# Gathering the first expert block's rows inside the routing block, and reordering the first pieces of the expert stage

## What is computed

```python
logits = h @ router_w + router_b
top_logit, top_e = lax.top_k(logits, 4)
top_w = softmax(top_logit)
# rows are sorted by expert and cut into blocks of 128 (each of one expert)
xb = h[buf_tok].reshape(n_blocks, 128, 1024)
def expert_block(xe, e):
    gate = minimum(xe @ w_gate[e] + b_gate[e], 7)
    up = clip(xe @ w_up[e] + b_up[e], -7, 7)
    act = (up + 1) * (gate * sigmoid(1.702 * gate))
    return act @ w_down[e] + b_down[e]
y = yb[dest] * sorted_w            # and summed back by token
x = x + g_m * moe(h)
```

## Time and profile before

| | |
|---|---|
| median of three runs | 2950.21 us |
| the profiled execution | 2950.6 us, its span 2948.8 us |
| TensorE busy | 2872.8 us (97% of the span) |
| VectorE busy | 2019.7 us (68%) |
| ScalarE busy | 1600.1 us (54%) |
| GpSimd busy | 551.3 us (19%) |
| expert stage | from 1680 us to the end |
| rate of the DMA engines in the expert stage | 381 to 388 GB/s in nearly every fortieth of the span |

### The profile page before, as it was taken

One profiled execution on the slowest core, in us unless ns is written; L12 is line 12 of the kernel. 1 busy time (PEld: TensorE's weight loads), 2 busy tenths in 40 slices (PEclk: granted clock), 3 DMA queues, 4 the chain that ended last, 5 costly groups with the idle time before them and its releaser, 6 DMA issues. The chain is left out here.

```text
span 2948.8 us, 41411 instructions
## 1 busy us (share of the span) xinstructions
PE 2872.8 (97%) x14988; PEld 2295.8 (78%) x14988; DVE 2019.7 (68%) x2273; ACT 1600.1 (54%) x1749; POOL 551.3 (19%) x479
## 2 busy tenths in 40 slices
PE   8999999998999999999999899999999999999999
PEld 4688888764788888876777688888888888888887
DVE  8642224587622236836753699999999999999998
ACT  5342323345522224434532577777777777777775
POOL 1012100113112100003100122322222222222331
PEclk9999999998999999999999999999999999999999
DMA  8422222220032232110022699999999999999995
GB/s 351 168 83 110 100 90 82 90 80 38 30 128 86 100 114 93 58 72 1 1 86 86 220 415 383 382 386 386 387 386 386 386 386 386 381 385 383 381 382 221
DMA packets 88924, 638.88 MB, mean 217 GB/s; under 512 B 10448, under 2 KB 11664, under 8 KB 26096
## 3 DMA queue, kind: packets, MB, share of 16 engines
q1 hardware_dynamic: 78592, 599.97, 51.9%
q0 software_dynamic: 9936, 36.75, 4.6%
q10 hardware_dynamic: 288, 0.65, 0.1%
HBM read 611.28 MB, written 26.05 MB: 216 GB/s over the span
## 5 line engine op out<-in xcount | busy, mean ns | idle before, releaser
L3208 DVE TENSOR_TENSOR arena_rounded<-arena,arena_rounded 128x2048 fp32r<-128x2048 f32 x420 | 951.1, 2286 | 90.6 <-ACT arena_rounded L3204 89.1
L3204 ACT ACTIVATE arena_rounded<-arena 128x2048 fp32r<-128x2048 f32 x420 | 801.3, 1918 | 209.4 <-PE banks L265 133.9
L263 PE MATMUL banks<-arena_rounded,operand_rounded 128*128 128x512 f32 (+1 forms) x2064 | 817.6, 396 | 4.2 <-DVE small_rounded L3500 2.2
L264 PE MATMUL banks<-arena_rounded,operand_rounded 128*128 128x512 f32 (+1 forms) x2064 | 801.6, 388 | 0.0
L265 PE MATMUL banks<-arena_rounded,operand_rounded 128*128 128x512 f32 (+1 forms) x1504 | 583.1, 388 | 0.0
L263 PEld LDWEIGHTS banks<-arena_rounded,operand_rounded 128*128 128x128 f32 x2064 | 387.8, 188 | 85.8 <-issue 4.7
L264 PEld LDWEIGHTS banks<-arena_rounded,operand_rounded 128*128 128x128 f32 x2064 | 388.1, 188 | 76.6 <-issue 1.0
L265 PEld LDWEIGHTS banks<-arena_rounded,operand_rounded 128*128 128x128 f32 x1504 | 282.4, 188 | 58.8
L263 PE MATMUL banks<-operand_rounded,arena_rounded 128*128 128x512 f32 (+2 forms) x712 | 268.0, 376 | 5.3 <-PE banks L265 5.2
L264 PE MATMUL banks<-arena_rounded,arena_rounded 128*128 128x512 f32 (+1 forms) x688 | 266.1, 387 | 0.0
L265 PE MATMUL banks<-operand_rounded,arena_rounded 128*128 128x512 f32 (+2 forms) x712 | 264.4, 371 | 0.0
(11 more groups left out here) (519 smaller groups left out, 3866.9 us busy)
## 6 DMA issues: line engine op xcount, KB each, us to landing
arena<-in_gate SPq DMA_DIRECT2D x140, 1024.0 KB, 7.5
arena<-in_up SPq DMA_DIRECT2D x140, 1024.0 KB, 7.7
arena<-in_down SPq DMA_DIRECT2D x140, 1024.0 KB, 6.1
arena<-in_dense SPq DMA_DIRECT2D x62, 2048.0 KB, 7.6
arena<-in_dense SPq DMA_DIRECT2D x6, 1024.0 KB, 5.1
small<-in_rows SPq DMA_DIRECT2D x7, 512.0 KB, 7.6
resid<-in_x SPq DMA_DIRECT2D x4, 512.0 KB, 8.2
expert_sums<-operand SPq DMA_DIRECT2D x4, 512.0 KB, 3.7
```

What stands on the lines that cost most here:

```text
L263: nc.tensor.matmul(out, left[0], right[0], start=start, stop=False)
L264: nc.tensor.matmul(out, left[0], right[1], start=False, stop=False)
L3204: nc.scalar.activation(high[q % NHI], raw[:, q, :], ACT.Copy).then_inc(high_ready, 1)
L3208: nc.vector.tensor_tensor(low[q], raw[:, q, :], high[q % NHI].bitcast(F32), ALU.subtract).then_inc(low_ready, 1)
```

## The change

- The semaphore of the first gather is made in the layout (`rows_in`), and `gather_rows` becomes a function of the module that takes the column as an argument.
- In `route`, VectorE writes `token` first and signals it with `numbered`; `filler` and `home` follow. GpSimd, at the end of its routing stream, waits for this and for the stores of the rows (`rows_out`), and gathers with `token`'s first column. In the expert stage it no longer loads `column`, copies `token_col` or gathers.
- ScalarE in the expert stage: `take_high` of piece 0, the four copies, both halves of `x_high`, then `take_high` of piece 1, then the one-element sigmoid with its table load, then piece 2.
- VectorE in the expert stage: `take_low` of piece 0 stands between the second and the third copy of bias sums.
- Two of the routing's semaphores become one (`weight`); counts on `staged` fall by one. TensorE's and SyncE's streams are unchanged but for the semaphore's name.

```diff
@@ route, vector
         dve.wait_ge(entered, ST)
         value = k.psum[:, 0, 0:P]
+        V.tensor_scalar(e["token"], value, float(S), float(S - 1), ALU.add, ALU.min).then_inc(numbered, 1)
         then(V.tensor_scalar(filler, value, 0.0, k.cst("pad"), ALU.is_equal, ALU.mult))
         V.scalar_tensor_tensor(out=e["home"], in0=value, scalar=float(S), in1=filler, op0=ALU.add, op1=ALU.add)
-        V.tensor_scalar(e["token"], value, float(S), float(S - 1), ALU.add, ALU.min)
@@ route, gpsimd
             i.then_inc(halved, 1)
+        pool.wait_ge(numbered, 2)
+        pool.wait_ge(rows_out, 16 * (ST + 1))
+        gather_rows(e, pool, e["token"][:, 0:1])
@@ experts, gpsimd
             last = last_block(pool)
-            column = pool.value_load(plan[0:1, NP:NP + 1], min_val=0, max_val=P - 1)
-            nc.gpsimd.tensor_copy(e["token_col"][:, 0:1], e["token"][:, bass.ds(column, 1)]).then_inc(staged, 1)
             nc.gpsimd.tensor_copy(e["choice"], k.cst("pick")[:, 0:1].broadcast_to([P, CAP])).then_inc(chosen, 1)
-            pool.wait_ge(staged, 1)
-            gather_rows(pool)
             pool.wait_ge(sums_out, 16 * ST)
@@ experts, scalar
-            nc.scalar.activation(table, table, ACT.Sigmoid).then_inc(y_ready, 1)
-            for q in range(2):
-                take_high(act, 0, q)
+            take_high(act, 0, 0)
             for t in range(ST):
                 act.wait_ge(biased, 2 * t + 1)
                 nc.scalar.activation(half(first_rows[t], 0), k.psum[:, first_bank(0, t), :], ACT.Copy).then_inc(biases_act, 1)
@@
             nc.scalar.activation(half(e["x_high"], 1), half(x_banks, 1), ACT.Copy).then_inc(x_high_ready, 1)
+            take_high(act, 0, 1)
+            nc.scalar.activation(table, table, ACT.Sigmoid).then_inc(y_ready, 1)
             for q in range(2, AHEAD):
                 take_high(act, 0, q)
@@ experts, vector
-            take_low(dve, 0, 0)
             for t in range(ST):
+                if t == ST // 2:
+                    take_low(dve, 0, 0)
                 dve.wait_ge(biased, 2 * t + 2)
                 V.tensor_copy(half(first_rows[t], 1), k.psum[:, first_bank(1, t), :]).then_inc(biases_dve, 1)
```

More of the change, by code:

```diff
@@ L2661, in expert_layout @@
     e["bias_in"] = k.nc.alloc_semaphore(name="expert_biases_in")
+    e["rows_in"] = k.nc.alloc_semaphore(name="expert_rows_in")
     e["in"] = [k.nc.alloc_semaphore(name=f"expert_weights_in_{n}") for n in range(PIECES)]
@@ L2670, in load_expert_piece, with gather_rows @@
     sp.dma_start(e["raw"][:, q, :], src[expert, half, part]).then_inc(e["in"][q], 16)
+def gather_rows(e, pool, column):
+    pool.indirect_dma_start(e["x_rows"], None, e["tokens_dram"],
+                            bass.IndirectOffsetOnAxis(ap=column, axis=0)).then_inc(e["rows_in"], 16)
 def route(k, e, fed):
@@ L2714, in route @@
     tokens = lambda t: slice(t * P, (t + 1) * P)
-    names = ("parts", "taken", "logits", "chain", "exp", "empty", "member", "ranked", "marked", "entered", "more", "more_turned",
+    names = ("parts", "taken", "logits", "chain", "weight", "empty", "member", "ranked", "marked", "entered", "more", "more_turned",
              "spread", "spread_turned", "spread_high", "rows_out", "turned_back", "copied",
-             "numbered", "halved", "weighed", "shared", "apart", "slotted", "bias_up", "bias_zero", "bias_high", "bias_low", "bias_out")
-    (parts_s, taken, logits_s, chain, exped, empty, member_s, ranked, marked, entered, more_s, more_turned,
+             "numbered", "halved", "shared", "apart", "slotted", "bias_up", "bias_zero", "bias_high", "bias_low", "bias_out")
+    (parts_s, taken, logits_s, chain, weight_s, empty, member_s, ranked, marked, entered, more_s, more_turned,
      spread_s, spread_turned, spread_high, rows_out, turned_back, copied,
-     numbered, halved, weighed, shared, apart_s, slotted, bias_up, bias_zero, bias_high, bias_low, bias_out) = (k.sem(f"route_{n}") for n in names)
+     numbered, halved, shared, apart_s, slotted, bias_up, bias_zero, bias_high, bias_low, bias_out) = (k.sem(f"route_{n}") for n in names)
     def sync(sp):
@@ L2759, in scalar @@
             copy_rows(n)
-        act.wait_ge(exped, 1)
-        nc.scalar.activation(weight, weight, ACT.Exp).then_inc(exped, 1)
+        act.wait_ge(weight_s, 1)
+        nc.scalar.activation(weight, weight, ACT.Exp).then_inc(weight_s, 1)
         for n in range(3, 2 * ST):
@@ L2858, in vector @@
         then(V.tensor_copy(index_3d(index_f), index[:, :, 0:NK]))
-        V.tensor_tensor(weight, best[:, :, 0:NK], best[:, :, 0:1].broadcast_to([P, ST, NK]), ALU.subtract).then_inc(exped, 1)
+        V.tensor_tensor(weight, best[:, :, 0:NK], best[:, :, 0:1].broadcast_to([P, ST, NK]), ALU.subtract).then_inc(weight_s, 1)
         then(V.tensor_tensor(chosen, iota.unsqueeze(1).broadcast_to([P, NA, NE]),
@@ L2864, in vector @@
         V.tensor_tensor(member[:, 0:ST, :], pairs[:, :, 0, :], pairs[:, :, 1, :], ALU.add).then_inc(member_s, 1)
-        dve.wait_ge(exped, 2)
+        dve.wait_ge(weight_s, 2)
         then(V.tensor_reduce(total, weight, AX.X, ALU.add))
         then(V.reciprocal(total, total))
-        V.tensor_tensor(weight, weight, total.unsqueeze(2).broadcast_to([P, ST, NK]), ALU.mult).then_inc(weighed, 1)
+        V.tensor_tensor(weight, weight, total.unsqueeze(2).broadcast_to([P, ST, NK]), ALU.mult).then_inc(weight_s, 1)
         dve.wait_ge(ranked, 1)
@@ L2941, in gpsimd @@
         nc.gpsimd.memset(e["spread_t"][0:2 * NE, :].bitcast(F32), 0.0).then_inc(bias_zero, 1)
-        pool.wait_ge(weighed, 1)
+        pool.wait_ge(weight_s, 3)
         nc.gpsimd.tensor_tensor(shares, chosen, e["weight"].unsqueeze(2).broadcast_to([P, NA, NE]), ALU.mult).then_inc(shared, 1)
@@ L3144, in experts @@
     GROUP = 4
-    plan, raw, low, high = e["plan"], e["raw"], e["low"], e["high"]
+    plan, raw, low, high, x_in = e["plan"], e["raw"], e["low"], e["high"], e["rows_in"]
     half = lambda x, h: x[:, h * NB:(h + 1) * NB]
-    names = ("x_in", "x_turned", "x_high_ready", "x_ready", "staged", "chosen", "used", "high_ready", "low_ready",
+    names = ("x_turned", "x_high_ready", "x_ready", "staged", "chosen", "used", "high_ready", "low_ready",
              "clipped", "opened", "gated", "hidden_ready", "hidden_turned", "hidden_high_ready", "hidden_split",
              "y_ready", "y_out", "passed")
-    (x_in, x_turned, x_high_ready, x_ready, staged, chosen, used, high_ready, low_ready, clipped, opened, gated,
+    (x_turned, x_high_ready, x_ready, staged, chosen, used, high_ready, low_ready, clipped, opened, gated,
      hidden_ready, hidden_turned, hidden_high_ready, hidden_split, y_ready, y_out,
@@ L3179, in block_number @@
                                   skip_runtime_bounds_check_because="only turns below the last block come here")
-    def gather_rows(pool):
-        pool.indirect_dma_start(e["x_rows"], None, e["tokens_dram"],
-                                bass.IndirectOffsetOnAxis(ap=e["token_col"][:, 0:1], axis=0)).then_inc(x_in, 16)
     def turn_rows(first=False):
@@ L3257, in _ @@
                             nc.gpsimd.tensor_copy(e["weight_next"], e["x_rows"][:, bass.ds(expert + D, 1)]).then_inc(staged, 1)
-                            pool.wait_ge(staged, 4 * b + 3)
+                            pool.wait_ge(staged, 4 * b + 2)
                             pool.sem_inc(passed, 1)
-                            gather_rows(pool)
+                            gather_rows(e, pool, e["token_col"][:, 0:1])
                             with pool.If(b > 0):
@@ L3268, in _ @@
                             pool.wait_ge(y_ready, b + 2)
-                            pool.wait_ge(staged, 4 * b + 5)
+                            pool.wait_ge(staged, 4 * b + 4)
                             pool.sem_inc(passed, 1)
@@ L3456, in _ @@
                             act.wait_ge(used, during(b, PIECES))
-                            act.wait_ge(staged, 4 * b + 5)
+                            act.wait_ge(staged, 4 * b + 4)
                             nc.scalar.activation(half(e["y"], 0), k.psum[:, 6, :], ACT.Copy, scale=e["weight_col"])
```

## The result

Over 20 runs each the changed kernel takes 2959.14 us against 2951.08 us: the ratio is 1.0026, with a 95% interval from 1.0018 to 1.0034. It is 8 us slower. The forecast was 1.1 us and a range that ended at 2953.4. The profiled execution has a span of 2957.4 us, 8.6 over the one before.

A forecast was written before the change was run, and what follows sets the result against it. TensorE was taken to bound all behind 1716 us, released by VectorE; 0.6 us for the later seam plus 0.5 for the table load's new place made 1.1 us, forecast 2951.3 us, range 2949.5 to 2953.4.

The forecast's parts named there:

- part 1: Routing block's end: GpSimd's gather there makes the streams go on 1.05 us later, TensorE's bias matmuls 0.62 us later.
- the end of the stage waits for the gather to land: Rival at the routing stage's end: the seam lies behind the gather's landing, +5.1 or +10 us; chance 0.04.
- The bound: From 1716 us TensorE is always busy, so a shift of its first down products (1715.24) reaches the end one for one.
- The chain to it through VectorE's packed pieces: Expert stage: VectorE, packed from 1696.99 to L3500, releases TensorE; piece 3 and all behind it come 1.1 us late.
- The place of the table load: ScalarE, expert stage: load and sigmoid, 1.39 us, fall between pieces 1 and 2, where ScalarE had 3.12 us idle.
- Part 3: VectorE and the bias-sum stores, expert stage: the last store lands by 1695.5 at worst, hidden by ScalarE's new work.
- parts 2 and 3: ScalarE's and VectorE's new order in the expert stage: the table load's new place costs 0.5 of the 1.1 us.
- The rival of a second stretch at the lower clock: TensorE idle 1.0 us at piece 1 lowers its clock again, about +2.4 us; chance 0.14 shared with longer gather and table drain.

The follow-up runs named there:

- plain-copy kernel: Kernel before, but GpSimd copies 128 token rows without indices at the routing block's end and gathers in the expert stage: 2959.01 us, ratio 1.0027.
- the gather alone: Changed kernel with ScalarE's and VectorE's edits undone, so only the gather moves to the end of GpSimd's routing stream: 2960.78 us, ratio 1.0033.

## Why the prediction was wrong

**The step that failed** is the one on the drain in part 1. It held that GpSimd arrives at the stage's end when it has written its descriptors, 1.20 us after the start, and took GpSimd's drain of 4.43 us beside computations as the evidence. That row could only show that the drain waits for instructions. No row of the kernel before had a DMA of GpSimd ahead of a stage end, and for this the nearest row was taken from SyncE, whose drain took 7 ns. The five kernels in which GpSimd had a DMA under way at the stage's end show what stands in its place: drain end against landing 1688.3 and 1688.3, 1697.7 and 1697.6, 1687.2 and 1687.2, 1688.1 and 1688.0, 1695.2 and 1695.1. The delay of the seam was 8.5 us and not 1.05.

**The rival** "the end of the stage waits for the gather to land" named the mechanism, its place and the wrong reassurance by SyncE's row, and was given 0.04. Its first price, +5.1 us, was too low as well, since it took the landing of 5.3 us of the old place; its second, +10 us with the median of 10.4, was nearer. At the new place, with 2 MB of SyncE's weights issued 1.1 to 1.6 us before, it is 9.2 us. With it the rival's own sum gives 1679.1 + 9.2 + 0.15 = 1688.5 and +8.5 us, less the 0.42 of bias wait and plus the 0.5 of the order: 8.6 us, the measured difference of the spans. That it fits to 0.1 us is in part luck: the bias matmuls start 7.9 us later and not 8.1, and take 0.2 us longer.

**What held.** The bound: TensorE behind 1716, full and one for one. The chain to it through VectorE's packed pieces. The moments of VectorE's first instruction and of its end, to 0.2 us, and the gather's 1.20 us; the gather started 0.3 us behind it instead of 0.67. The place of the table load: it stood ahead of the sigmoid, between two pieces, and cost VectorE 1.0 us of idle time. Part 3: the stores hold nothing (ScalarE's wait for them is gone), and removing the stall gives nothing, since the load took its place. The sum of parts 2 and 3 was 0.5, and from the first product on all five kernels with that order take 0.5 us more than the one before. The rival of a second stretch at the lower clock, behind the new idle time at piece 1, did not come: TensorE was idle for 0.79 us ahead of 1702.45, and the granted clock is 1.00 from 1700 to 1726.

**The two places from the Trainium skill.** "ScalarE: Activation LUTs", section "What ACT_TABLE_LOAD costs", has a drain of some 1380 ns with each load. With ScalarE at work directly ahead (1698.16 + 1.92), the load starts at 1700.09 and the next activation at 1701.39, 1.30 us later: no drain on either side, as in rows 4. "SBUF — State Buffer", section "SBUF: two separate sides", speaks of VectorE's two-port kind only, and the prediction took VectorE's last instructions for that kind without a row for it. The gather started at 1679.11 with one of them under way (1678.84 to 1679.19), one more and two copies to come, and took no longer than with VectorE idle, so these did not hold it.

**What was left open.** The clock stood at its lower level from 1680 to about 1693.6 in the changed kernel. It fell when TensorE had been idle since 1678.5, stayed low for the rest of the 11 us of idle time, and rose with TensorE at work since 1689.55:

```profile
1680.00:1682.00 2.00, 0.00 (x0) 0.00 (x0) 0.00 (x0) 0.00 (x0) 0.31 (x1) 0.50 1.03 287
...
1692.00:1694.00 2.00, 2.00 (x7) 1.58 (x6) 0.98 (x2) 0.60 (x1) 0.00 (x0) 0.60 0.32 129
```

It cost little against before, where part of them ran at that level too (rows 10): the 16 bias matmuls took 5.75 us instead of 5.53. How the DMA engines share between SyncE's and GpSimd's transfers isn't settled; 4 MB and 2 MB ahead gave the same landing, none ahead half of it.

## What to carry to other kernels

Don't let GpSimd issue a DMA as the last thing ahead of a stage's end, be it a gather or a plain copy: its drain lasts until the landing and all engines wait for it, while SyncE's drain beside 2 MB in flight took 7 ns. Issue it behind the seam; here the rows then landed 0.7 us later and the stage began 8.6 us sooner, both counted from VectorE's first instruction. Before moving a transfer earlier, see whether its landing follows its own issue at all; here it followed SyncE's. When a trace has no row for an edit (this engine's drain behind this kind of transfer), a row of another engine says nothing of it, and a rival without a row against it deserves more than 0.04.

## What the runs showed of the hardware

- GpSimd's drain ended within 0.1 us of the landing of its DMA in all five kernels, at 4.5 to 9.2 us of landing; SyncE's took 7 ns with 2 MB in flight.
- A transfer of 0.5 MB by GpSimd landed after 9.0 to 9.2 us when issued within 2 us of the first of 2 or 4 MB of weight loads by SyncE, after 7.8 and 7.0 us when issued 3.2 and 3.9 us behind it, and after 6.2, 5.8 and 5.3 us when 4.8, 5.4 and 5.8 us behind it: each time 10.7 to 11.2 us after that first load's issue. With none of them under way a gather landed after 4.5 us, and after 4.4 us as the second transfer of the plain-copy kernel.
- An activation table load took 1.28 us between two activations, with the next one 0.02 us behind it.
- The 16 bias matmuls took 5.2 to 6.6 us in the ten traces; in the longest (the gather alone) the granted clock was 0.50 until 1704.5, while TensorE had been at work again since 1698.9, behind 10.9 us of idle time.
